# The up matrix of each expert block loaded through ScalarE's DMA queue

## What is computed

```python
def expert_block(args):
    toks, ws, e = args
    xb = u_pad[toks]
    hid = jax.nn.silu(xb @ we_gate[e]) * (xb @ we_up[e])
    return (hid @ we_down[e]) * ws[:, None]
```

## Time and profile before

| | us |
|---|---|
| median of 3 runs | 2885.08 (2883.0 to 2885.61) |
| the profiled execution | 2896.94 |
| its span, first to last instruction | 2894.9 |
| PE busy | 2614.2 (90% of the span) |
| ScalarE busy | 655.1 (23%) |
| DMA queue q1 (SP), whole run | 342.27 MB, 33.2% of 16 engines |
| DMA queue q10 (ScalarE), whole run | 4.19 MB, 0.4% |
| loop over the routed blocks | 2120.36 to 2847.5 |

### The profile page before, as it was taken

The page is one execution under the profiler, slowest core; times in us unless marked ns, Lnnn a source line. Parts: engine busy times, 40 slices in busy tenths (PEclk is TensorE's granted clock), DMA queues, the critical chain, the costliest instruction groups (busy, mean ns, idle before and its releaser), DMA issues.

```text
span 2894.9 us, 25467 instructions
## 1 busy us (share of the span) xinstructions
PE 2614.2 (90%) x8938; PEld 1524.9 (53%) x8938; DVE 1111.9 (38%) x2005; ACT 655.1 (23%) x1084; POOL 538.1 (19%) x442
## 2 busy tenths in 40 slices
PE   5999996899999889999998899986889999999995
PEld 3885345678777533445454444574444444444443
DVE  4545333499851332445555321124611111111113
ACT  3334243333332222222222110222111111111111
POOL 2330003234333200000000001130322322222220
PEclk8997678899999899899999799997989999999998
DMA  3222000155632022211112011212089999999995
GB/s 117 75 88 87 1 0 30 58 175 181 214 122 102 0 87 83 66 44 44 56 46 87 30 58 58 87 33 80 31 324 304 343 339 314 353 331 332 324 321 147
DMA packets 163575, 403.43 MB, mean 139 GB/s; under 512 B 12128, under 2 KB 88928, under 8 KB 139552
## 3 DMA queue, kind: packets, MB, share of 16 engines
q1 hardware_dynamic: 142896, 342.27, 33.2%
q0 software_dynamic: 19440, 55.79, 8.0%
q10 hardware_dynamic: 1152, 4.19, 0.4%
HBM read 378.62 MB, written 39.32 MB: 144 GB/s over the span
## 4 chain that ended last, share of the span: by engine, by line
PE 78%; DVE 9%; DMA 7%; issue 2%; ACT 2%; POOL 1%; POOLq 0%; SPq 0%; DVEq 0%; ACTq 0%
PE bank L644 42%; PE bank L653 19%; DMA arena<-u_rows,rows_in 4%; PE bank L811 3%; PE bank L751 2%; PE bank L728 2%; PE bank L1078 2%; PE bank L670 2%; PE bank L918 1%; DVE hn L1594 1%; DMA arena<-in_w_up 1%; PE bank L742 1%; DVE arena L1725 1%; PE bank L732 1%; DVE inv L1591 1%
## 5 line engine op out<-in xcount | busy, mean ns | idle before, releaser
L644 PE MATMUL bank<-arena 128*128 128x512 f32 x1840 | 812.6, 598 | 8.6 <-DVE arena L1940 5.8
L644 PEld LDWEIGHTS bank<-arena 128*128 128x128 f32 x1840 | 348.2, 192 | 421.2 <-issue 417.1
L644 PE MATMUL bank<-hn,arena 128*128 128x512 f32 (+1 forms) x1168 | 530.8, 614 | 13.7 <-ACT hn L1161 10.6
L644 PEld LDWEIGHTS bank<-hn,arena 128*128 128x128 f32 (+1 forms) x1168 | 225.2, 195 | 298.7 <-issue 282.5
L2060 DVE TENSOR_TENSOR arena<-arena,bank 128x256 f32<-128x256 f32 x62 | 26.1, 421 | 501.6 <-ACT arena L1554 501.6
L603 POOL DMA_INDIRECT y_rows<-arena,rows_out x62 | 98.8, 1594 | 504.8 <-DVE arena L2072 271.2
L653 PE MATMUL bank<-x_high,w_high 128*128 128x512 f32 x352 | 141.1, 401 | 14.1 <-DVE x_low L1601 13.0
L560 POOL TENSOR_TENSOR pooled_low<-arena,pooled_high 128x512 fp32r<-128x512 f32 x8 | 9.9, 1266 | 742.8 <-ACT pooled_high L1473 742.8
L653 PE MATMUL bank<-x_low,w_high 128*128 128x512 f32 x352 | 139.7, 397 | 0.0
L653 PE MATMUL bank<-x_high,w_low 128*128 128x512 f32 x352 | 139.7, 397 | 0.0
L2072 DVE TENSOR_SCALAR arena<-bank,arena 128x512 f32<-128x512 f32 x124 | 93.1, 751 | 115.8 <-PE bank L644 115.8
(11 more groups left out here) (307 smaller groups left out, 3919.1 us busy)
## 6 DMA issues: line engine op xcount, KB each, us to landing
arena<-in_we_gate SPq DMA_DIRECT2D x62, 1024.0 KB
arena<-in_we_up SPq DMA_DIRECT2D x62, 1024.0 KB
arena<-in_we_down SPq DMA_DIRECT2D x62, 1024.0 KB, 8.7
arena<-in_w_in SPq DMA_DIRECT2D x30, 1024.0 KB, 5.9
arena<-in_w_ada SPq DMA_DIRECT2D x12, 2048.0 KB, 8.1
arena<-in_w_up SPq DMA_DIRECT2D x22, 1024.0 KB, 11.3
arena<-in_w_in SPq DMA_DIRECT2D x17, 512.0 KB, 4.2
arena<-in_w_out SPq DMA_DIRECT2D x4, 2048.0 KB, 8.1
```

The source lines that it names most:

```text
L644: ins = nc.tensor.matmul(out, w(k), rhs(k), start=first and k == 0, stop=last and k == nk - 1)
```

## The change

SP issues only the gate matrix in `load_up`. A function of the same name in ScalarE's program reads the block's expert itself and issues the up matrix, same destination, same source, same semaphore. ScalarE calls it for blocks 0 and 1 ahead of everything in this stage, and then in the loop: the up matrix of block 2i after the Silu of block 2i - 2 and ahead of the copies of block 2i, and likewise for 2i + 1. It has no wait of its own; the Silu ahead of it in ScalarE's program has waited for the product that frees the buffer.

```diff
--- before.py
+++ after.py
@@ -466,10 +466,8 @@
                 e = sp.value_load(expert_of[0:1, bass.ds(b, 1)], min_val=0, max_val=E - 1)
                 if freed:
                     sp.wait_ge(S("moe_gu"), *freed)
-                for name, half in (("we_gate", 0), ("we_up", 1)):
-                    sp.dma_start(moe["gu"][:, p, half * KD * FE:(half + 1) * KD * FE],
-                                 A[name][bass.ds(e, 1)].rearrange("a (p k) n -> p (a k n)", k=KD))\
-                      .then_inc(S(f"up_in{p}"), 16)
+                sp.dma_start(moe["gu"][:, p, 0:KD * FE], A["we_gate"][bass.ds(e, 1)].rearrange("a (p k) n -> p (a k n)", k=KD))\
+                  .then_inc(S(f"up_in{p}"), 16)
 
             def load_down(b, p, *freed):
 
@@ -1557,13 +1555,26 @@
             pairs_but_one = act.value_load(expert_of[0:1, MAX_BLOCKS:MAX_BLOCKS + 1], min_val=TT * TOP // 2 - 1,
                                             max_val=MAX_BLOCKS // 2 - 1)
             pairs = pairs_but_one + 1
+            def load_up(b, p):
+
+                e = act.value_load(expert_of[0:1, bass.ds(b, 1)], min_val=0, max_val=E - 1)
+                act.dma_start(moe["gu"][:, p, KD * FE:2 * KD * FE],
+                              A["we_up"][bass.ds(e, 1)].rearrange("a (p k) n -> p (a k n)", k=KD))\
+                   .then_inc(S(f"up_in{p}"), 16)
+
+            for p in range(2):
+                load_up(p, p)
             block_rows(0, 0)
             block_rows(1, 1)
             block_gate(0, 0)
             with act.Fori(1, pairs) as i:
-                for b, p in ((i * 2 + (-1), 1), (i * 2, 0)):
-                    block_rows(b + 1, 1 - p)
-                    block_gate(b, p)
+
+                load_up(i * 2, 0)
+                block_rows(i * 2, 0)
+                block_gate(i * 2 + (-1), 1)
+                load_up(i * 2 + 1, 1)
+                block_rows(i * 2 + 1, 1)
+                block_gate(i * 2, 0)
             block_gate(pairs_but_one * 2 + 1, 1)
             squares("n6", lambda k: (S("h_done"), 4 * KD + k + 1))
```

## The result

The changed kernel takes 2900.55 us in the median of 7 runs (2894.64 to 2909.72), the kernel before, timed beside it, 2881.21 us in the median of 7 (2878.25 to 2885.61). The ratio is 1.0071 with a 95% interval of 1.0050 to 1.0091: slower by 0.7%, as was forecast (2903 us). The profiled executions are 2907.27 us after and 2896.94 before.

The account below looks back on a forecast made before the run. It took PE and the DMA engines as both full in the routed-expert loop, which is sensitive to the gather's landing. Loop +15 us and start +2.5 us made about +18 us on 2885: 2903 us, range 2874 to 2934 us.

Parts of the forecast that it names:

- The place: Routed-expert loop: the gather's landing is where the kernel is sensitive; 7.15 us would cost nothing, the median gather takes 7.0.
- Steps 1 to 3: SP's dropped issue, ScalarE's added load and issue (about 0.9 us a block, hidden by idle time), no new wait: 0 us.
- Step 4: Up matrix issued about 0.7 us behind the gate but wanted some 16 us on: 0 us.
- Step 5: Third queue beside late gather rows: turn grows from 0.43 to 0.74 us, ordinary gathers +0.5 us; together +15 us.
- The three long ones: Gathers where an engine trails by 4 to 5 us: three at 2.2 us more each, 6.6 us.
- the clock: Longer PE stalls in the loop lower the clock more often: +2 us.
- Step 6: Start: the first two gathers run against full weight queues, with nothing to hide it: +2.5 us.
- The signs: Trace values named beforehand to show the forecast right or wrong: q10's share, gather times, PE's waits, block times, ScalarE's copies.
- The sum: All steps together: about +18 us, 2885 + 18 = 2903 us.
- Nothing happens: Rival: up queue flows only after ordinary gathers have landed, bytes and packets the same; 2885 us, +-5; chance 22%.
- Weight packets get longer: Rival: gate and up read at the same time stretch packets by 10%; 2925 to 2940 us; chance 8%.
- It gets faster: Rival: two queues shorten the lagging engine's weight packets; 2870 us, at most 2857; chance 13%.

Follow-up runs that it names:

- experiment 1: Each gather sent one scatter earlier: on the kernel before 2864.47 us, ratio 0.9935; on the changed kernel 2867.28 us, ratio 0.9941.
- experiment 2: Kernel before plus ScalarE's load of the expert's number and an 8-byte DMA issue per block, weights all on SP's queue: 2891.21 us, ratio 1.0033.
- experiment 5: Kernel before, one weight queue, SP issuing gate and up only after VectorE has used the product's result: 2905.17 us, ratio 1.0061.
- experiment 4: Kernel before, one weight queue, SP issuing the up matrix behind the down matrix: 2973.28 us, ratio 1.0297.
- experiment 7: Changed kernel with ScalarE waiting for the product itself and issuing the up matrix ahead of the Silu: 2892.04 us, ratio 1.0017.
- experiment 9: Changed kernel with the up matrices of blocks 0 and 1 issued by SP: 2882.49 us in one execution, not timed repeatedly.
- experiment 8: Each weight load split into two of 4 KB runs: kernel before 2916.96 us, ratio 1.0115; changed kernel 2935.59 us, ratio 1.0160.

## Why the prediction was right, and where it was not

- **The place.** Right: the gather's landing is what the loop is sensitive to. With the gather out of the way the two kernels are equal within their intervals (experiment 1), and the traces show no wait for weights.
- **Steps 1 to 3** (SP's issue, ScalarE's time, no new wait): nothing in the traces speaks against their 0 us. The copies keep their 3.71 us of cover, and the load takes 0.28 us, not 0.46. But the 0.3% of experiment 2 are not explained, so "0 us" for ScalarE's work is not fully shown.
- **Step 4, which puts the later issue of the up matrix at 0 us, has the wrong reason.** It asked only whether the matrix comes in time for its product. It does, but a later issue also pushes weights into the time of the scatter, and the gather goes behind it: 0.9 us of delay of two matrices on one queue costs 18 us (experiment 5), 4.1 us of delay of the up matrix 85 us (experiment 4). How much of the changed kernel's loss is due to this is open. Its delay is 0.36 us of one matrix in the mean; an estimate in proportion to experiments 5 and 4 gives 4 to 8 us of the 19, and the count of weight packets beside the scatter (16 against 12) points to a small share as well.
- **Step 5, the turn**: right in size, 0.77 against 0.46 us (forecast 0.74 against 0.43), wrong in its bill. Ordinary gathers did not get 0.5 us longer: the median stayed at 7.0 us, and was 0.2 us up where nothing fed back. The three long ones did not get 2.2 us longer; there were five instead of three. Longer waits less what the DMA catches up were put at 13 us and came to 5.6; the clock was put at 2 us and cost 4.6. So the loop lost 10.1 us in the trace where 15 were forecast. That the turn costs time in the loop by itself is not shown: experiment 7 has some of the turns (5 gaps of 0.77 us) and hardly the loss.
- **Step 6, the start**: +2.5 us forecast, +2.7 measured, and with one queue it goes away (experiment 9).
- **The signs.** As named: a third of the weights on q10, unhindered blocks at 11.4 us, copies at once. Not as named: the gather's median stayed at 7.0 us (7.3 to 7.6), its longest in the loop was 11.8 us (over 12), and PE waited 12 times for 26.4 us (more than 14 times, 30 us or more). By these signs the forecast's mechanism is only half confirmed.
- **The sum**, 18 us, stands beside 19.3 us between the medians of the timed runs and 10.3 between the profiled executions, which vary more than that step by step. It was right as a whole by a mechanism that was only partly the right one: that a gather bill set too high and a delay set at nothing come out so near to 19 us is luck.
- **The rivals.** "Nothing happens": no, by the interval. The Trainium skill, "DMA: Bandwidth & Descriptors", section "Issuing engines are not separate DMA queues", says that DMAs started by several engines share the same 16 DMA engines. This trace agrees: the queues' shares add up to 41.4% against 41.6%. The section is silent on who waits, and the 0.7% lies there. "Weight packets get longer": no; by the records of the single packets an 8 KB packet of the loop takes 0.346 us in the mean after and 0.344 before, the slow ones included. "It gets faster": no, though the fastest executions of two queues reach those of one.

**Open**: how the loss divides between the later issue (0.36 us in the mean), the turns of a second queue, and ScalarE's new work acting through the gather; what the 0.3% of experiment 2 are; and why the one execution of experiment 9 was so short. A kernel that delays only the up matrix by 0.36 us on SP's queue was not tried, and neither was one with ScalarE issuing the up matrix at exactly SP's old time.

## What to carry to other kernels

When the DMA engines are full, the question to ask of a moved load is not only whether it lands in time for its own use, but beside what it will flow: here 0.9 us of delay of loads that are wanted 16 us after their issue and land after 6 to 9 cost 18 us, through a gather that shared the engines. A second issuing queue gave no bandwidth here, and it took a share of the turns from the transfers that are on the path (0.77 us between trailing rows in place of 0.46). The cheaper cure is to take the sensitive transfer off the path: one gather sent a scatter earlier gave back about 19 us and made the kernel indifferent to which queue loads the up matrix.

## What the runs showed of the hardware

- Weight packets of 8 KB take 0.31 us as a rule. But just before the scatter flows, 1 to 2.5 us behind GpSimd's issue of the gather, about half of those then in flight take over 0.4 us (0.52 in the median), in both kernels. In the order of the queue they are the down matrix's. Of the up matrix's packets on q10 in the changed kernel's loop, some 7600, only 101 are so slow. What slows them was not tested.
- An adding scatter's row of 4 KB takes 0.33 us, twice a gathered row's 0.16.
- Weights in runs of 4 KB kept the engines busy 6.8% longer for a MB than in runs of 8 KB (experiment 8).
- PE's stalls cost more than their own length, since the granted clock fell to 1.2 GHz beside the longer ones (17 us of the loop before, 27 us of the changed one). In the profiled loops that is nearly half of what the change costs.
